# Retention scores of the next two heads issued in one visit with the value products of these two

## The reference, cut to what matters

```
h    = rms_norm(x, norm_mix_g)
rq, rk, rv, rg, aq, ak, av = split(h @ w_in)           # rv, rg: 2048 columns each
scores[n, m] = (rq[n] . rk[m]) * gamma_h^|n-m| / sqrt(128)   # 0 where chunk(m) > chunk(n), chunks of 64
ret  = scores @ rv                                     # per head
ret  = silu(rg) * ret * rsqrt(mean(ret^2) + eps) * ret_norm_g
y_ret = ret @ w_ret_branch
```

## Time and profile before

| | |
|---|---|
| median of 3 runs | 1502.2 us (1502.08 to 1502.4) |
| the profiled execution | 1502.11 us |
| its span, first to last instruction | 1500.1 us |
| outside the span | 2.01 us |
| mean granted TensorE clock | 0.999 of full speed |
| PE busy / PE weight loads busy | 1489.5 / 1287.8 us |
| DVE busy / ACT busy / POOL busy | 1030.5 / 791.5 / 39.4 us |

### The profile page before, as it was taken

How to read it: one execution, slowest core, us unless ns; L and a number is a source line. 1 busy time by engine, 2 the same in 40 slices (tenths; PEclk the granted TensorE clock), 3 DMA queues, 4 the chain that set the end, 5 groups by cost and what they waited for, 6 DMA issues and landing times.

```text
span 1500.1 us, 19036 instructions
## 1 busy us (share of the span) xinstructions
PE 1489.5 (99%) x7016; PEld 1287.8 (86%) x7016; DVE 1030.5 (69%) x1395; ACT 791.5 (53%) x1049; POOL 39.4 (3%) x52
## 2 busy tenths in 40 slices
PE   9999999999999999999999999999999999999997
PEld 7888888888888888888888888888888888888886
DVE  7987987555556877777799877338754586438845
ACT  6555555444444454454445565555655556555553
POOL 0000000000000000000000000000000000000000
PEclk9999999999999999999999999999999999999999
DMA  9545545666655565666665888987889888888883
GB/s 326 194 159 168 183 153 171 201 208 213 230 186 179 196 216 175 197 196 224 212 228 205 235 259 270 266 256 221 255 274 264 239 238 273 250 259 249 238 267 116
DMA packets 154120, 331.83 MB, mean 221 GB/s; under 512 B 5584, under 2 KB 5712, under 8 KB 149840
## 3 DMA queue, kind: packets, MB, share of 16 engines
q1 hardware_dynamic: 149024, 297.51, 58.2%
q0 software_dynamic: 4464, 32.51, 11.7%
q10 hardware_dynamic: 576, 1.06, 0.2%
HBM read 296.45 MB, written 2.10 MB: 199 GB/s over the span
## 4 chain that ended last, share of the span: by engine, by line
PE 96%; DVE 2%; issue 1%; DMA 0%; ACT 0%; POOL 0%; POOLq 0%; DVEq 0%; ACTq 0%
PE acc L434 92%; DVE wlo L1013 1%; PE tps L449 1%; PE pps L476 1%; PE pps L459 0%; DVE kT L1022 0%; DVE qT L1022 0%; PE sps L467 0%; PE acc L490 0%; DMA raw<-in_w_in 0%; DVE ta_lo L1443 0%; PE tps L586 0%; PE tps L584 0%; PE tps L585 0%; DVE final L1455 0%
## 5 line engine op out<-in xcount | busy, mean ns | idle before, releaser
L686 ACT ACTIVATE whi<-raw 128x1024 fp32r<-128x1024 f32 x542 | 567.0, 1054 | 546.2 <-PE acc L434 542.4
L1013 DVE TENSOR_TENSOR wlo<-raw,whi 128x1024 fp32r<-128x1024 f32 x480 | 582.9, 1224 | 359.6 <-ACT whi L686 356.0
L434 PE MATMUL acc<-whi,ta_hi 128*128 128x512 f32 x1308 | 501.3, 383 | 0.8 <-DVE wlo L1013 0.8
L434 PE MATMUL acc<-whi,ta_lo 128*128 128x512 f32 x1308 | 495.7, 379 | 0.0
L434 PE MATMUL acc<-wlo,ta_hi 128*128 128x512 f32 x1180 | 447.2, 379 | 0.0
L434 PEld LDWEIGHTS acc<-whi,ta_hi 128*128 128x128 f32 x1308 | 247.1, 189 | 43.0 <-issue 4.8
L434 PE MATMUL acc<-whi,tb_hi 128*128 128x512 f32 x736 | 279.3, 380 | 0.0
L434 PE MATMUL acc<-whi,tb_lo 128*128 128x512 f32 x736 | 278.9, 379 | 0.0
L434 PEld LDWEIGHTS acc<-whi,ta_lo 128*128 128x128 f32 x1308 | 247.2, 189 | 35.1
L434 PEld LDWEIGHTS acc<-wlo,ta_hi 128*128 128x128 f32 x1180 | 223.1, 189 | 30.6 <-issue 0.3
L434 PE MATMUL acc<-wlo,tb_hi 128*128 128x512 f32 x616 | 233.5, 379 | 0.0
(11 more groups left out here) (141 smaller groups left out, 824.7 us busy)
## 6 DMA issues: line engine op xcount, KB each, us to landing
raw<-in_w_in SPq DMA_DIRECT2D x66, 1024.0 KB, 5.2
raw<-in_w_up SPq DMA_DIRECT2D x64, 1024.0 KB, 5.8
raw<-in_w_down SPq DMA_DIRECT2D x64, 1024.0 KB, 6.4
raw<-in_w_gate SPq DMA_DIRECT2D x32, 1024.0 KB, 5.4
low<-raw POOLq DMA_DIRECT2D x31, 1024.0 KB, 8.1
raw<-in_w_att SPq DMA_DIRECT2D x16, 1024.0 KB, 5.0
raw<-in_w_ret SPq DMA_DIRECT2D x16, 1024.0 KB, 5.0
raw<-in_w_out SPq DMA_DIRECT2D x16, 1024.0 KB, 5.4
```

Source lines behind the costliest of these rows:

```text
L434: last = nc.tensor.matmul(paired(acc[B.parity][:, t, :]), a[:, k, tok], halves_in_turn(b), start=(k == 0 and n == 0), stop=(k == KCH - 1 a ...
L686: nc.scalar.activation(whi[:, s:s + UCH, :], raw[:, u * UCH:(u + 1) * UCH, :], ACT.Copy).then_inc(hi_ready, 1)
L1013: V_.tensor_tensor(wlo[:, s:s + UCH, :], raw[:, u * UCH:(u + 1) * UCH, :], whi[:, s:s + UCH, :].bitcast(f32), ALU.subtract).then_inc(lo_re ...
```

## The change

PE's score visit is split from its value visit in the source (`retention_scores`, `retention_values`). In turn 0 the scores of turn 0 stay where they were. In turns 0 to 2 the scores of turn j+1 stand right behind the value products of turn j, between G4 and G5. In turns 1 to 3 there is no score visit between G1 and G2 any more. So the score and value products form 5 visits instead of 8. ACT copies the keys one turn earlier (`keys_of`). DVE multiplies with the mask of turns 1 to 3 in `tail3`, between units V0 and V1, instead of between G5 and G6. PE's and ACT's loops run over turns 1 and 2, and turn 3 is straight code; DVE's loop still has three turns.

```diff
--- before.py
+++ after.py
@@ -560,13 +560,10 @@
                 gemm(Block(B2 + 1, 2, j), tb_hi, tb_lo, 0, 8)
 
 
-            def stage3(j, first):
-                V, G = Block(B3, 2, j), Block(B3 + 1, 2, j)
-                gemm(V, ta_hi, ta_lo, 0, 8)
-                gemm(G, ta_hi, ta_lo, 0, 2)
+            def retention_scores(j):
 
                 pe.wait_ge(kst_ready, j + 1)
-                if not first:
+                if later(j):
                     pe.wait_ge(ptr_ready, j * 2)
                 for i in range(2):
                     q = qkT[:, ds(j * 2 + i, 1), :].rearrange("p a n -> p (a n)")
@@ -574,10 +571,12 @@
                     nc.tensor.matmul(rs_ps[i][:, S:RET_COLS], kst[:, i, P:S],
                                      qkT[:, ds(j * 2 + i, 1), P:S].rearrange("p a n -> p (a n)"),
                                      start=True, stop=True).then_inc(rs_full, 1)
-                gemm(G, ta_hi, ta_lo, 2, 5)
+
+            def retention_values(j, V):
+
                 pe.wait_ge(evacuated[1], V.turn + 1)
                 pe.wait_ge(ptr_ready, j * 2 + 2)
-                if not first:
+                if later(j):
                     pe.wait_ge(ret_read, j)
                 for i in range(2):
                     v = [buf[0][:, t, i * RET_V:(i + 1) * RET_V] for t in range(TILES)]
@@ -585,11 +584,23 @@
                     nc.tensor.matmul(out_ps[:, i, 1, :], ptr[:, i, P:S], v[0], start=True, stop=False)
                     last = nc.tensor.matmul(out_ps[:, i, 1, :], ptr[:, i, S:RET_COLS], v[1], start=False, stop=True)
                 last.then_inc(ret_full, 1)
+
+            def stage3(j, more=True):
+                V, G = Block(B3, 2, j), Block(B3 + 1, 2, j)
+                gemm(V, ta_hi, ta_lo, 0, 8)
+                gemm(G, ta_hi, ta_lo, 0, 2)
+                if not later(j):
+                    retention_scores(j)
+                gemm(G, ta_hi, ta_lo, 2, 5)
+                retention_values(j, V)
+                if more:
+                    retention_scores(j + 1)
                 gemm(G, ta_hi, ta_lo, 5, 8)
 
-            stage3(0, True)
-            with pe.Fori(1, 4) as j:
-                stage3(j, False)
+            stage3(0)
+            with pe.Fori(1, 3) as j:
+                stage3(j)
+            stage3(3, False)
 
 
             def stage4(j, first):
@@ -869,27 +880,38 @@
                 scaled(Block(B3 + 1, 2, j), buf[2], ACT.Tanh, rstd_half).then_inc(rgate_ready, 1)
                 split(B, 4, 8)
 
-            def stage3(j, first):
+            def keys_of(j):
+
+                nc.scalar.activation(kst[:], qkT[:, ds(j * 2 + RET_HEADS, 2), :], ACT.Copy).then_inc(kst_ready, 1)
+
+            def stage3(j, more=True):
                 V, G = Block(B3, 2, j), Block(B3 + 1, 2, j)
-                if first:
+                if not later(j):
                     split(V, 0, 8)
                     act.wait_ge(r_placed, 8)
+                    keys_of(0)
                 else:
                     tail3(j - 1, V)
-                    act.wait_ge(rs_full, j * 2)
-                nc.scalar.activation(kst[:], qkT[:, ds(j * 2 + RET_HEADS, 2), :], ACT.Copy).then_inc(kst_ready, 1)
+                    if more:
+                        act.wait_ge(rs_full, j * 2 + 2)
+                        keys_of(j + 1)
                 split(G, 0, 2)
-                if not first:
+                if later(j):
                     hi_from_gained(j + (T_STAGE3 - 1), buf[2], tb_hi, j - 1)
                 split(G, 2, 4)
-                if not first:
+                if later(j):
                     act.wait_ge(ret_full, j)
                 scaled(V, buf[0], ACT.Copy, rstd).then_inc(evacuated[1], 1)
-                split(G, 4, 8)
-
-            stage3(0, True)
-            with act.Fori(1, 4) as j:
-                stage3(j, False)
+                split(G, 4, 6)
+                if not later(j):
+                    act.wait_ge(rs_full, 2)
+                    keys_of(1)
+                split(G, 6, 8)
+
+            stage3(0)
+            with act.Fori(1, 3) as j:
+                stage3(j)
+            stage3(3, False)
 
 
             def stage4(j, first):
@@ -1277,9 +1299,12 @@
             mine.leave_loop(3, OWN_STAGE2)
 
 
-            def tail3(j, B):
-
-                split(B, 0, 2)
+            def tail3(j, B, more=False):
+
+                split(B, 0, 1)
+                if more:
+                    decayed(j + 1)
+                split(B, 1, 2)
                 dve.wait_ge(rssq_ready, j + 1)
                 V_.tensor_scalar(msq[:], ssqr[:].rearrange("p i t -> p (i t)"), 1.0 / RET_V, EPS, ALU.mult, ALU.add).then_inc(rms_ready, 1)
                 split(B, 2, 3)
@@ -1327,10 +1352,11 @@
                     dve.wait_ge(decay_full, 16)
                     split(G, 0, 2)
                 else:
-                    tail3(j - 1, V)
+                    tail3(j - 1, V, True)
                     after3(j - 1, G)
                 split(G, 2, 6)
-                decayed(j)
+                if first:
+                    decayed(j)
                 split(G, 6, 8)
 
             stage3(0, True)
```

## The result

The changed kernel is slower by a little: 1504.07 us in the median of 22 runs (1503.51 to 1505.59), against 1502.32 us of 22 runs of the kernel before. The ratio is 1.0012, with a 95% interval of 1.0006 to 1.0017. The forecast was 1502.1 in a range up to 1503.1.

The account below looks back on a forecast made before the run. PE, busy 99% of the span and without gaps in stage 3, was taken to bound the kernel. 1502.11 - 0.05 (merge) + 0 (keys, mask, cover, loops) = 1502.06, against the median 1502.15; forecast 1502.1, range 1501.2 to 1503.1.

Parts of the forecast that it names:

- What bounds the kernel, and what a visit costs: Stage 3: PE bounds without gaps; turns 45.34 us, value visit 2.59, score visit 1.31 with only 0.015 beyond its columns.
- The predicted 0.05 us: PE in stage 3: gain from three score visits losing their edges, three times 0.015 us.
- The rival with a price of 0.2 us a visit: PE's visits have a fixed price, saved three times: 0.6 us gained, 1501.5 us, turn 45.1; chance 0.09.
- The keys and the mask: ACT's key copy (0.61 us) and DVE's mask (about 1.0 us) in stage 3 fit into idle time and cost nothing.
- The slower rival by DVE's mask: DVE's mask blocks V1 in turns 1 to 3: 2.5 us a turn if nothing hid it, 1509.6 in all; chance 0.02.
- The cover that goes: Between G1 and G2, turns 1 to 3: losing 1.31 us of cover leaves G2 3.3 us to spare; no PE wait.
- Every sign that the prediction named for its forecast: Stage 3: 192 full matmuls between merged visits of 3.90 us, 45.34 us turns, mask about 0.7 us behind, no PE wait.
- the length of the span: Whole kernel: a span more than 3 us away from 1500.1 would make the prediction wrong.
- Loops: PE and ACT in stage 3: turn 3 as straight code, one return less, no cost either way.
- the Trainium skill's rule on branches: PE's loop in stage 3: a taken branch outside the window stalls; one such stop would go, size not given.
- The rival "supply of instructions": New order or straight turn on PE in stage 3 costs one to two 0.4 us stops, 1502.5 to 1502.9; chance 0.06.
- The range: Whole kernel: 1501.2, from the visit's price with run spread, to 1503.1, from two 0.4 us stops with spread.

Follow-up runs that it names:

- e2: Changed kernel with PE's order kept but stage 3's loop cut elsewhere as three turns, nothing duplicated: 1502.24 us against 1502.23, ratio 1.0.
- e1: Kernel before in its old order, with only PE's turn 3 of stage 3 written out as straight code: 1504.09 us, ratio 1.0012.
- e3: Changed kernel with 84 more instructions (long-met waits) ahead of the MLP's loop on PE, its head at 6753: 1502.51 us, ratio 1.0002.
- e4: Kernel before with 172 long-met waits ahead of the MLP's loop on PE, its head at 6413: 1504.54 us, ratio 1.0015.
- e7: Kernel before with 203 long-met waits ahead of the MLP's loop on PE, its head at 6444: 1502.75 us, ratio 1.0004.
- e9: Changed kernel with the MLP's loop on PE written out, so no return to a loop's head there: 1502.44 us, ratio 1.0001.
- e5: Kernel before with 189 long-met waits ahead of the MLP's loop on PE, its head at 6430: 1507.40 us, ratio 1.003.
- e6: Kernel before with 130 long-met waits ahead of the MLP's loop on PE, its head at 6371: 1504.04 us, ratio 1.0013.

## Why the prediction was wrong

**What bounds the kernel, and what a visit costs: right.** Stage 3's turns are 45.34 us before and after, the merged visit is 3.90 us as summed, and e2 puts the worth of the merge at 0.0 us with an interval of 0.9991 to 1.0009. The predicted 0.05 us can't be told from it. The rival with a price of 0.2 us a visit has no support: its turn of 45.1 us didn't appear.

**The keys and the mask: right.** The wait on ACT was 0.25 us (predicted 0.2), the mask starts 0.81 us behind the value products (0.7) and V1's `wlo` 5.03 us behind them (5.0), with ACT as releaser. The slower rival by DVE's mask didn't happen.

**The cover that goes: right.** No PE wait in stage 3. Every sign that the prediction named for its forecast appeared. Apart from the length of the span, 2.3 us more where 3 were allowed, none of them looks beyond stage 3.

**Loops: this is the step that failed.** I wrote "no cost either way", on the ground that turns reached from straight code and from a return are equally long. That compares returns inside a loop of 450 instructions. It says nothing on a loop of 1619 that lies elsewhere, and the straight turn's 428 instructions moved that one, so that its return took 4.11 us instead of 0.21 and PE stood still twice. I had named the Trainium skill's rule on branches, but had looked for its effect only at the loop that was edited, and so got its sign wrong: I had it take a stop away. The measured term is the stretch behind stage 3, 1.94 us in the profile, 1.75 in the medians.

**The rival "supply of instructions" was the nearest**, with the right kind of cause, the wrong place (the new straight code) and too small a price (one or two stops of 0.4 us, from the earlier trace rows). It had 0.06. The range ended at its price, so it missed the time by 1.0 us.

Shown by runs: that the straight turn alone makes the slowdown (e1), that the order alone makes none (e2), that the place of the loop decides (e3, e4, e7), that no return means no stop (e9), and, by the traces, that the loop's second turn fetches nine packets in every kernel with a stop and none in the others with the loop. Not settled: why the return's branch lasts anything between 3.5 and 5.2 us, and with it the first stop and the price of a return to within about 2 us. That the room is eight blocks, one of them always filled ahead, and that a boundary lies at 39 past, fits all eleven kernels but is inferred: no view shows the room or its boundaries.

## What to carry to other kernels

Where PE's list holds a loop of more than six blocks of 256 instructions, an edit ahead of it can be an edit of that loop too: count the instructions that the edit adds, and look at the length of the return's branch, at the packets of the instruction queue behind it and for "issue" in the chain there. A peeled turn isn't free because its own stretch is; cutting the loop at another place (e2) gave the same order without it. A difference of 0.1% behind a reordering should be sought over the whole span before the reordering is blamed.

## What the runs showed of the hardware

- On the TensorE queue a return to a loop of 1619 instructions costs at most some 0.5 us (e2, e3, e7) or 1.7 to 5.1 us, by the loop's place alone (e7 and e5, 14 instructions apart: 1502.75 and 1507.40 us). The branch itself lasts 0.21 us or 3.5 to 5.2 us.
- When the loop doesn't fit, it is fetched again: 9 packets of 16 KB between the return and the loop's last branch in all six such kernels, none in the four others that have the loop.
- From the restart at the head to the restart at the next block 3.81 us pass in the changed kernel (1161.59 to 1165.40), 3.95 in e1 and 3.02 in e5. Matmuls left in the head's block hide part of it or all: 12 of them left a second stop of 0.97 to 1.33 us (changed kernel, e1, e4), 3 left 2.11 (e5), and with 34 of them, 7.3 us by count, e6 has none.
- Stops of 0.70 and 2.11 us with three matmuls between were followed by seven matmuls at a granted clock of 0.52 (e5); stops of 0.47 and 0.97 us with twelve between left it at 1.00 (changed kernel).
- The Trainium skill ("Runtime: NRT & Kernel Launch", Instruction fetch mechanics) speaks of a window of two pages for a branch. For PE these runs disagree: a loop that touches seven blocks returns without a stop and without a packet. The room of 2048 instructions, eight blocks, that is cited above fits them.
- A float32 visit of 128-row products among the projections costs its columns and nothing more: 3.90 us for 16 records of 256 columns (3.453) and 4 of 128 (0.432), which leaves 0.015.
